# A decoder layer on one core: five stage borders with another order on ScalarE, VectorE and TensorE

## What is computed

```
h = rmsnorm(x, g_mix_pre);  z = h @ w_in                       # latents, pool input, two gates
y_a = mla(...) @ w_attn_br;  y_p = pool(...) @ w_pool_br
merged = sigmoid(gate_a) * y_a + sigmoid(gate_p) * y_p
x = x + rmsnorm(merged @ w_mix_out, g_mix_post)
h = rmsnorm(x, g_mem_pre);  mem_n = rmsnorm(mem, g_mem_kv)
x = x + rmsnorm(memory_xattn(h, mem_n, w_mem_q, w_mem_kv, w_mem_o), g_mem_post)
h = rmsnorm(x, g_ffn_pre)
x = x + rmsnorm(conv_gated_ffn(h, w_ffn_in, conv_w, conv_b, w_ffn_out), g_ffn_post)
```

## Time and profile before

| | |
|---|---|
| runs | 1782.45, 1782.66, 1782.91 us; median 1782.66 |
| profiled execution | 1782.73 us, span 1781.0 us |
| TensorE busy | 1766.4 us (99% of the span) |
| VectorE, ScalarE busy | 1171.0 us (66%), 938.0 us (53%) |
| granted TensorE clock | 0.999 over the span |
| DMA | 330.78 MB, mean 186 GB/s |

### The profile page before, as it was taken

The page is one execution under the profiler, slowest core; times in us unless marked ns, Lnnn a source line. Parts: engine busy times, 40 slices in busy tenths (PEclk is TensorE's granted clock), DMA queues, the critical chain, the costliest instruction groups (busy, mean ns, idle before and its releaser), DMA issues.

```text
span 1781.0 us, 25260 instructions
## 1 busy us (share of the span) xinstructions
PE 1766.4 (99%) x8854; PEld 1481.9 (83%) x8854; DVE 1171.0 (66%) x1644; ACT 938.0 (53%) x1280; POOL 60.4 (3%) x128
## 2 busy tenths in 40 slices
PE   9999999999999999999999999999999999999998
PEld 7888888888887888888888878888888888888786
DVE  5555565655455655544555477777888887788887
ACT  7555565565545554444555474444444444455554
POOL 4000000000000110000000100000000000000002
PEclk9999999999999999999999999999999999999999
DMA  8456454554556555555444556555555555656555
GB/s 289 154 189 183 152 185 134 184 163 159 207 193 233 196 187 188 187 177 187 155 143 173 188 179 215 189 188 186 185 184 185 185 185 187 200 174 211 182 200 189
DMA packets 192239, 330.78 MB, mean 186 GB/s; under 512 B 17286, under 2 KB 43318, under 8 KB 190774
## 3 DMA queue, kind: packets, MB, share of 16 engines
q1 hardware_dynamic: 190630, 318.48, 54.4%
q10 hardware_dynamic: 1552, 11.54, 1.7%
HBM read 325.81 MB, written 4.19 MB: 185 GB/s over the span
## 4 chain that ended last, share of the span: by engine, by line
PE 95%; DVE 2%; ACT 1%; issue 1%; DMA 0%; DVEq 0%; SPq 0%; ACTq 0%
PE bank L1039 17%; PE bank L596 15%; PE bank L598 14%; PE bank L597 14%; PE bank L1041 9%; PE bank L1087 4%; PE bank L1089 4%; PE bank L1088 4%; PE bank L907 3%; PE bank L908 2%; PE bank L770 2%; PE bank L621 1%; PE bank L771 1%; DVE wlo L1691 1%; PE bank L793 1%
## 5 line engine op out<-in xcount | busy, mean ns | idle before, releaser
L1691 DVE TENSOR_TENSOR wlo<-raw,whi 128x1024 fp32r<-128x1024 f32 x520 | 637.5, 1229 | 526.7 <-ACT whi L1198 378.1
L1198 ACT ACTIVATE whi<-raw 128x1024 fp32r<-128x1024 f32 x376 | 397.9, 1059 | 461.3 <-PE bank L598 245.7
L1039 PE MATMUL bank<-actA,whi 128*128 128x512 f32 x1344 | 472.1, 394 | 0.0
L1041 PE MATMUL bank<-actA,wlo 128*128 128x256 f32 x1344 | 380.2, 283 | 0.0
L1039 PEld LDWEIGHTS bank<-actA,whi 128*128 128x128 f32 x1344 | 252.4, 188 | 58.3
L596 PE MATMUL bank<-whi,actA 128*128 128x512 f32 x672 | 272.2, 405 | 2.0 <-DVE wlo L1691 1.1
L598 PE MATMUL bank<-whi,actA 128*128 128x512 f32 x672 | 265.4, 395 | 0.0
L597 PE MATMUL bank<-wlo,actA 128*128 128x512 f32 x672 | 265.0, 394 | 0.0
L1041 PEld LDWEIGHTS bank<-actA,wlo 128*128 128x128 f32 x1344 | 252.7, 188 | 0.0
L1184 ACT ACTIVATE whi<-raw 128x1024 fp32r<-128x1024 f32 (+1 forms) x144 | 150.5, 1049 | 137.6 <-PE bank L598 84.4
L596 PE MATMUL bank<-whi,actB 128*128 128x512 f32 x448 | 178.3, 398 | 0.5 <-DVE actB L1706 0.3
(11 more groups left out here) (286 smaller groups left out, 2053.3 us busy)
## 6 DMA issues: line engine op xcount, KB each, us to landing
raw<-in_w_ffn_in SPq DMA_DIRECT2D x88, 1024.0 KB
raw<-in_w_in SPq DMA_DIRECT2D x48, 1024.0 KB
raw<-in_w_ffn_out SPq DMA_DIRECT2D x84, 512.0 KB, 4.8
raw<-in_w_mem_kv SPq DMA_DIRECT2D x32, 1024.0 KB
raw<-in_w_attn_br SPq DMA_DIRECT2D x16, 1024.0 KB
raw<-in_w_mix_out SPq DMA_DIRECT2D x16, 1024.0 KB
raw<-in_w_mem_q SPq DMA_DIRECT2D x16, 1024.0 KB
raw<-in_w_mem_o SPq DMA_DIRECT2D x16, 1024.0 KB
```

The costliest lines, as they stand in the source:

```text
L1039: pe.matmul(dst[:, :], whi[:, s, o:o + P], actA[:, :, kt, :], start=(kt == 0), stop=False)
L1041: mm = pe.matmul(dst[:, 0:S], wlo[:, s, o:o + P], actA[:, 0, kt, :], start=False, stop=(kt == KD - 1))
L1198: act.activation(whi[:, ks % AHEAD, 0:w], raw[:, c, ks % 2, 0:w], ACT.Copy).then_inc(hi_done, 1)
L1691: dve.tensor_tensor(wlo[:, vs % AHEAD, 0:w], raw[:, c, vs % 2, 0:w], f32(whi[:, vs % AHEAD, 0:w]), ALU.subtract).then_inc(lo_done, 1)
```

## The change

It moves work in the queues and adds or removes no operation. In column 0 of the mixing product ScalarE squares two quarters each at k = 0 and 1 and none at k = 6. In column 1 the fills and splits of the memory tokens go from k = 2, 3, 4, 5, 6, 6, 7, 7 to k = 1, 2, 3, 4, 5, 6, 7, 7. In the last key column VectorE sums the first half before the low part of k = 6. In the last head VectorE splits the head's output before the low part of k = 5. At the border into the feed-forward part, TensorE's fills 2, 3, 4 and 5 come one half unit later and fills 6 and 7 one unit earlier, ScalarE does S(0) between H(0) and H(1), and x3_square(0) before the second root, and VectorE does L(3) before the norm of the second half and R(1,1) after D(2). In the last product step 4 of `combine` moves ahead of a low part.

```diff
@@ -329,7 +329,7 @@
 
     X3_ORDER = ((0, 0), (1, 0), (0, 1), (1, 1), (2, 0), (2, 1), (3, 0), (3, 1))
 
-    X3_FILL = ((0, 2), (0, 3))
+    X3_FILL = ((0, 3), (1, 0))
 
     def x3_at(j, t):
         return 8 + X3_ORDER.index((j, t)) + 1
@@ -876,7 +876,7 @@
             merged(ND - 1)(k)
 
         def mem_job(k):
-            for f in ((), (), (0,), (1,), (2,), (3,), (4, 5), (6, 7))[k]:
+            for f in ((), (0,), (1,), (2,), (3,), (4,), (5,), (6, 7))[k]:
                 pe.wait_ge(mem_ok, 2 * (f // 2) + 2)
                 t_fill(T_MEM + f, f, memv_words, 2 * f)
 
@@ -1044,6 +1044,9 @@
 
         def ffn_turn(i, first):
             for k in range(4 if first else 0, 16):
+                if first and k == 4:
+                    x3_fill(6)
+                    x3_fill(7)
                 if first and k in (4, 6):
                     pe.wait_ge(t_out, T_X3 + k + 2)
                 if first and k < 8:
@@ -1054,9 +1057,6 @@
                     if not first and k == 8:
                         pe.wait_ge(uconv, 2 * i)
                     turned(V_FIN + 16 * i + k, k, k // 8, k % 8)
-                if first and k == 4:
-                    x3_fill(6)
-                    x3_fill(7)
                 if first and k == 9:
                     a_fill()
                     r_fill()
@@ -1072,7 +1072,7 @@
                     mm.then_inc(w_used, 1)
                 if (t, k) in X3_FILL:
                     x3_fill(X3_FILL.index((t, k)) + 2)
-                if t == 1 and k == 0:
+                if t == 1 and k == 1:
                     x3_fill(4)
                     x3_fill(5)
         ffn_turn(0, True)
@@ -1426,7 +1426,7 @@
         def mem_squares(k):
             if k == 0:
                 act.wait_ge(mem_in, 16)
-            for q in (k,) if k < 6 else (6, 7) if k == 6 else ():
+            for q in ((0, 1), (2, 3), (4,), (5,), (6,), (7,), (), ())[k]:
                 square(N_MEM, q, memv[:, q % 2, q // 2 * NC:(q // 2 + 1) * NC])
             merged(ND - 1)(k)
             if k == 2:
@@ -1553,15 +1553,15 @@
         square_of(N_Y2, 0)
         root_of(N_Y2, 0)
         hi_at(V_MO, ND - 1, 8, 4)
+        x3_split(0)
         hi_at(V_MO, ND - 1, 8, 5)
-        x3_split(0)
         x3_split(1)
         hi_at(V_MO, ND - 1, 8, 6)
         act.wait_ge(w_used, V_MO + 8 * ND)
         square_of(N_Y2, 1)
         hi_at(V_MO, ND - 1, 8, 7)
+        x3_square(0)
         root_of(N_Y2, 1)
-        x3_square(0)
         x3_square(1)
         x3_split(2)
         x3_square(2)
@@ -1968,7 +1968,10 @@
                         keys = memk[:, 4 * n + 2 * b:4 * n + 2 * b + 2, :]
                         dve.tensor_tensor(keys, keys, psum[:, first[b]:first[b] + 2, S:2 * S],
                                           ALU.add).then_inc(keys_sum, 1)
-                lo_at(V_MKV, n, 8, k)
+                        if n == ND - 1 and b == 0:
+                            lo_at(V_MKV, n, 8, 6)
+                if n < ND - 1 or k != 6:
+                    lo_at(V_MKV, n, 8, k)
                 job(k)
 
         for n in range(ND):
@@ -2034,7 +2037,7 @@
             elif k != 6:
                 mem_head(ND - 1)(k)
 
-        column(V_MO, 0, last_head, (0, 3, 4))
+        column(V_MO, 0, last_head, (0, 3, 4, 5))
         with dve.Fori(1, ND - 1) as n:
             column(V_MO, n, nothing)
 
@@ -2070,13 +2073,13 @@
         lo_at(V_MO, ND - 1, 8, 5)
         x3_split(1)
         lo_at(V_MO, ND - 1, 8, 6)
+        lo_at(V_MO, ND - 1, 8, 7)
         variance_of(N_Y2, 1)
         rstd_of(N_Y2, 1)
         x3_residual(0, 1)
-        lo_at(V_MO, ND - 1, 8, 7)
-        x3_residual(1, 1)
         last_gain(1, bufY, gpost)
         x3_split(2)
+        x3_residual(1, 1)
         x3_residual(2, 0)
         x3_residual(2, 1)
         x3_split(3)
@@ -2286,8 +2289,8 @@
             if n in (12, 13, 15, 16):
                 xs_make(0, G0, 7 + (12, 13, 15, 16).index(n), 0)
             if n in (FORM_END[0] + 1, FORM_END[0] + 2):
-                for i in range(3):
-                    combine(0, 3 * (n - FORM_END[0] - 1) + i + 1)
+                for i in ((1, 2, 3, 4), (5, 6))[n - FORM_END[0] - 1]:
+                    combine(0, i)
             if n == START[1]:
                 combine(0, 7)
                 combine(0, 8)
@@ -2298,8 +2301,8 @@
             if START[1] + 3 < n <= START[1] + 7:
                 xs_make(G0, G1, n - START[1] + 3, 1)
             if n in (FORM_END[1] + 1, FORM_END[1] + 2):
-                for i in range(3):
-                    combine(1, 3 * (n - FORM_END[1] - 1) + i + 1)
+                for i in ((1, 2, 3, 4), (5, 6))[n - FORM_END[1] - 1]:
+                    combine(1, i)
         dve.wait_ge(gpost_in, 16 * 3)
         dve.wait_ge(x3_in, 16)
```

## The result

The changed kernel took 1786.91 us (median of 15 runs, 1785.24 to 1788.28), the kernel before 1783.14 us in the same comparison (15 runs, 1782.39 to 1785.04). The ratio is 1.0019, 95% interval 1.0012 to 1.0026. That lies in the range and in the case "within 0.2%", but the median is 3.8 us above before, not 2.7. The fastest runs of the two stand 2.85 us apart. Both facts want an explanation, and so does the place of 1786.91 in the range, 0.09 us under its upper end.

The account below looks back on a forecast made before the run. TensorE bounds the kernel, busy 1766.4 of 1781.0 us, leaving only its short waits to change. Terms summed to +2.69 us on 1782.73 (1785.42, or 1785.35 from the median), stated as 1785.4, +0.15%; range 1783.7 to 1787.0.

Parts of the forecast that it names:

- the range: Forecast time of the whole kernel: 1783.7 to 1787.0 us, leaving out the clock and the faster case.
- within 0.2%: Case for the whole kernel: its time differs from before by no more than 0.2%; chance 0.83.
- squares: Mixing product, column 0: TensorE's whole wait for ScalarE's accumulator copy goes, -0.60 us.
- second mixing column: Mixing product, column 1: fill 0 waits for the scaled memory tokens, +1.48 us; the last fills' wait goes, -0.42.
- keys: Last key column: VectorE's sum of the first half starts earlier, so TensorE follows earlier, -0.24 us.
- last head: Last head: VectorE's split starts earlier, so unit 6 starts earlier, -0.15 us.
- border into the feed-forward part: Largest term: delayed fills and VectorE's residuals make TensorE wait, +2.50 us, between 2.0 and 3.3 at the ends.
- combinations: Last product: step 4, now next to step 3 which it needs, loses an overlap, +0.12 us.
- The sum's own band: Whole kernel: the summed terms hold as they stand, 1784.6 to 1786.1 us; chance 0.65.
- more slips in the chain of fills: Rival at the feed-forward border: a second square or a load is late, 1786.2 to 1787 us; chance 0.14.
- the first rival: Clock falls in the new feed-forward gap: one unit at the lower level gives 1788.2 us, two 1791.0; chance 0.05.
- The queue sums of the border: Feed-forward border, expected before each part's run: fills 2 to 5 +3.8 us, VectorE +1.5, ScalarE -0.3, fills 6 and 7 +0.4.

Follow-up runs that it names:

- e3: Kernel before with only the squares, the keys' low part, the last head's low part and the combinations moved; 1781.10 us.
- e1: Kernel before with only the table of the memory tokens' splits and fills moved, on all three engines; 1783.54 us, before beside it 1782.94.
- e2: Kernel before with only the edits at the border into the feed-forward part, on all engines together; 1786.40 us.
- e5: Kernel before with only TensorE's fills 2 to 5 at the feed-forward border one multiplication group later; 1788.36 us, before 1782.58.
- e9: The changed kernel again, unedited, timed beside the kernel before; median 1786.84 us, 1.0022 of before, 11 runs.
- e8: Kernel before with only fills 6 and 7 at the feed-forward border put ahead of unit 4; 1785.98 us.
- e12: Kernel before with small moves, six combinations in one step, memory fills 3 and 4 together, ScalarE's first split moved, VectorE's split of 2 ahead of last gain; 1779.85 us, 0.9982.
- e10: The changed kernel with idle transposes of the identity on TensorE in its two gaps; median 1785.08 us, 1.0010 of before, 11 runs.
- e6: Kernel before with only VectorE's order at the feed-forward border changed: low part 7 before the norm, residual (1,1) after the split of 2; 1784.05 us.

## Why the prediction was right, and where it was short

Every wait that the prediction lists for the new profile appeared, and the steps have these sizes:

| step | predicted | changed kernel | alone |
|---|---|---|---|
| squares | -0.60 | -0.61 | -0.56 (e3) |
| second mixing column | +1.48 - 0.42 | +1.10 | +1.00 (e1) |
| keys | -0.24 | -0.26 | -0.32 (e3) |
| last head | -0.15 | -0.18 | -0.16 (e3) |
| border into the feed-forward part | +2.50 | +2.47 | +4.09 (e2), 1.6 of it the clock |
| combinations | +0.12 | +0.19 | +0.14 (e3) |
| sum | +2.69 | +2.71 | |

The chain at the large border holds link by link, too. VectorE's timeline of the changed kernel has R(0,1) and the pair R(3,0), R(3,1):

```profile
1042.50 0.75 DVE L1951 SCALAR_TENSOR_TENSOR bufX<-bufY,rstd,bufX 128x512 f32<-128x512 f32 x1
...
1054.49 1.41 DVE L2050 SCALAR_TENSOR_TENSOR bufX<-bufY,rstd,bufX 128x512 f32<-128x512 f32 x2
```

Less the 1.65 us by which TensorE is late ahead of this border, they start at 1040.85 and 1052.84 (predicted 1040.90 and 1052.85), and t1k0 at 1044.71 (predicted 1044.7). One figure on record doesn't follow from the others: t1k0 "at about 1045.3 there with the earlier terms in". The earlier terms sum to +0.07, which makes it 1044.8.

**The sum holds where the clock does.** With the gaps filled, the median is 1785.08 us, where the prediction said 1785.4; against the before of the same comparison it is +2.3 by medians and +2.7 by the fastest runs. The fastest runs of the changed kernel stand 2.85 and 2.95 us above those of before. What the orders cost is thus 2.3 to 3.0 us, around the predicted 2.7.

**That the median lies in the range is partly luck.** The sum's own band was 1784.6 to 1786.1, and 1786.91 lies above it, in the band up to 1787 that was kept for more slips in the chain of fills (chance 0.14). No such slip came. What filled the band was the lower clock, the case that the range says it leaves out, and a kernel before that stood at 1783.14 in this comparison, 0.48 us over the median that the sum starts from.

**The step that failed is the first rival.** "The granted clock was 1.00 in a stretch of 5 us in which TensorE worked for 0.86 us, so a gap of 2.5 us should not cost it": the row was right and my reading of it wrong. In the idle stretch of e2 at 1042 the clock also stands at 1.00; it shows lower only in the next stretch, when TensorE works again. The stretch behind the earlier trace rows is this one in the kernel before:

```profile
1777.00:1781.00 4.00, 0.00 (x0) 0.64 0.72 243
```

So the trace of before did hold a fall behind idle time, one row further on. It comes over 4 us behind TensorE's last matmul (start 1772.47), so it doesn't say that 2.4 us are enough; but neither does say that they aren't. The price was off as well: I took a whole unit at the lower level, 2.8 us, and it was 1.6, since the clock came back after some 3 us. The Trainium skill ("TensorE: Matmul & The Clock Gate", section on HAM oscillation) describes a kernel in which TensorE waits for a DMA between its bursts, falls back to the lower clock and starts each burst with it. Its waits are longer than the gap here; three of the four profiles with the unfilled gap of 2.39 us (e2, e5, e9) show a fall all the same, and the changed kernel's first does not. I had given this 0.05, and e9's run times, eight of eleven at 1786.7 or more, suggest that it happens in most executions. The mean granted clock of each run points the same way. Of the fourteen profiles the six at 0.999 hold no fall ahead of the last matmul, the three at 0.997 hold one or two, and 0.998 goes with none or one. Of e9's runs the three fastest ran at 0.999, the next four at 0.998 and the four slowest at 0.997. The medians' distance of 3.8 and 4.1 us is 2.7 us of order plus, in some executions, the clock: 1.6 us for one fall, 2.9 for the two in e9's profile (5.35 less 2.47). How much of it falls at the border and how much at the start-up isn't shown.

**The start-up is a second, separate term, and not the change's.** The changed kernel's first profile lost 1.7 us before any moved instruction, and 1.7 of its 4.7 us are this. It is the lower clock again, and not the wait for the input by itself. TensorE's timeline of the kernel before:

```profile
6.66 2.78 PE L645 MATMUL bank<-ident 128*128 128x128 f32 x12
```

and of the changed kernel:

```profile
6.67 1.50 PE L645 MATMUL bank<-ident 128*128 128x128 f32 x12
9.79 0.87 PE L621 MATMUL bank<-ident_r,bufX_words 128*128 128x128 f32 x8 [1.61 <-DMA bufX<-in_x]
```

The same 12 transposes took 2.78 us in one and 1.50 in the other. Where they were quick, TensorE stood 1.61 us for the second lot of input tokens. That lot began only 0.27 us later (9.52 before), but behind the gap the matmuls started 0.43 us apart, with a granted clock of 0.60 and 0.55 in the stretches 11 to 13 and 13 to 15 us. So the profile that was quicker ahead of the input lost more behind it. e8's 2.84 us are both, a second lot that began at 10.69 and the lower clock behind it. e12 shows the same in its profile; its timeline of TensorE at the second lot:

```profile
9.55 0.87 PE L621 MATMUL bank<-ident_r,bufX_words 128*128 128x128 f32 x8 [1.66 <-DMA bufX<-in_x]
10.86 0.47 PE L596 MATMUL bank<-whi,actA 128*128 128x512 f32 x1 [0.45 <-DVE wlo L1691]
11.17 0.45 PE L597 MATMUL bank<-wlo,actA 128*128 128x512 f32 x1
11.42 0.63 PE L598 MATMUL bank<-whi,actA 128*128 128x512 f32 x1
```

Its profiled run took 1781.46 us and nine others 1779.7 to 1780.0. The kernel before has the same tail: 9 of its 35 runs are over 1783.5, with 26 from 1782.07 to 1783.23. Five of these 9 ran at a mean clock of 0.997, none of the 26 did, so in those five the clock probably fell somewhere. That it fell at the start-up isn't shown, since none of the 9 has a trace.

**The queue sums of the border hold one by one but don't add.** Predicted and measured: fills 2 to 5 +3.8 and +3.9 (clock taken out), VectorE +1.5 and +1.8, ScalarE -0.3 and -0.3, fills 6 and 7 +0.4 and +0.6. The four measured parts sum to +5.9, and together they cost 2.5: with the fills moved but VectorE's order left as it was, e5 has another wait of 1.3 us for line 1691 in TensorE's list, which the whole change doesn't have.

**Left open.** Why the clock falls behind the same gap in one execution and not in another: the rows ahead of the gap are alike in e9 and in the changed kernel's first profile. Also the drift of 0.4 us behind 1661 in that profile alone; e9 and e10 don't have it.

## What to carry to other kernels

- At a hand-written border follow the queues of all three engines link by link, with durations from rows. Each engine's order is a bet on the others': a moved step costs what it now waits for, and parts of one reordering don't add. Include the write-after-read waits (an accumulator that somebody must have read first), which my last sum left out.
- A gap on TensorE is worth its idle time, and in some executions the lower clock behind it. Look for the fall in the stretch behind the gap, where work goes on: a row of idle time at 1.00 doesn't show that the clock stays. Where a gap of 2 us can't be closed, idle transposes in it can keep the clock and narrow the spread of the runs (here from 5.7 to 0.75 us, 11 runs each).
- Where one profile and one median differ by more than the sum, split the offset by place first. Here 1.7 of 4.7 us lay ahead of the change.

## What the hardware showed that I had not expected

- Behind an idle time of 2.39 us on TensorE the granted clock fell to the lower level in three profiles of four, for about 3 us, and cost some 1.6 us; behind 1.95 us it fell once (e9), and behind 1.31 us at the memory fill, 0.97 and 1.59 in e6, 1.56 in e2 and 1.54 at the changed kernel's fills 6 and 7 it did not. At the start-up it fell behind 1.6 to 1.7 us (changed kernel, e12) and, in e8, behind 1.3 us with another 0.55 behind it.
- TensorE's loss by the clock made the next gap longer in e9: 1.95 us before fills 6 and 7, where the profile without a fall has 1.54. TensorE's timeline of e9:

```profile
1049.29 0.80 PE L621 MATMUL bank<-ident_r,bufX_words 128*128 128x128 f32 x8
1049.95 0.50 PE L596 MATMUL bank<-whi,actA 128*128 128x512 f32 x1
...
1054.96 1.41 PE L621 MATMUL bank<-ident_r,bufX_words 128*128 128x128 f32 x8 [1.95 <-DVE bufX L2050]
```

  From fills 4 and 5 to fills 6 and 7 it is 5.67 us here and 5.68 in the changed kernel's first profile (1049.61 to 1055.29): the chain over ScalarE and VectorE between them is as long in both. But t1k2 starts 0.66 us behind fills 4 and 5 here and 1.09 there, where it still waits 0.29 us for D(3). At the lower clock TensorE came to fills 4 and 5 later behind fill 3 (2.41 us against 1.75), D(3) was ready, that wait went, and the time stood at the next one.
